# One layer pair on one core: gated one-hots on GpSimd, the sparse token tile chosen second, 111 row operations in the u loop, and an address strip in the expert stage

## The reference

```python
# experts: rows sorted by expert and padded to blocks of 128
def expert_block(args):
    xe, e = args
    gu = xe @ w_gate_up[e] + b_gate_up[e]
    g = jnp.minimum(gu[:, :D_FF], SWIGLU_LIMIT)
    u = jnp.clip(gu[:, D_FF:], -SWIGLU_LIMIT, SWIGLU_LIMIT)
    act = (u + 1.0) * (g * jax.nn.sigmoid(SWIGLU_ALPHA * g))
    return act @ w_down[e] + b_down[e]

# PEER: 8 heads choose 16 of 128 x 128 = 16384 experts per token
best_s, pos = lax.top_k(cand_s, PEER_TOPK)
expert_idx = jnp.take_along_axis(cand_i, pos, axis=-1)
gates = jax.nn.softmax(best_s, axis=-1)
u_sel = u_tab[i_blk]
act = jax.nn.gelu(jnp.einsum('td,thkd->thk', h_blk, u_sel).astype(jnp.float32))
w = (g_blk * act).astype(h.dtype)
return jnp.einsum('thk,thkd->td', w, v_tab[i_blk])
```

## Time and profile before

| | us |
|---|---|
| median of three runs | 3818.42 (3814.71 to 3826.18) |
| the profiled execution | 3818.46 |
| its span | 3816.6 |
| PE busy | 3387.5 (89%) |
| DVE busy | 2730.8 (72%) |
| ACT busy | 1932.5 (51%) |
| POOL busy | 607.7 (16%) |
| expert stage | from about 588 to 1815 |
| u loop | from about 2540 to 3222 |
| v loop | from about 3232 to 3802 |

### The profile page before, as it was taken

How to read it: one execution, slowest core, us unless ns; L and a number is a source line. 1 busy time by engine, 2 the same in 40 slices (tenths; PEclk the granted TensorE clock), 3 DMA queues, 4 the chain that set the end, 5 groups by cost and what they waited for, 6 DMA issues and landing times. The chain is left out here.

```text
span 3816.6 us, 46791 instructions
## 1 busy us (share of the span) xinstructions
PE 3387.5 (89%) x16253; PEld 2821.9 (74%) x16253; DVE 2730.8 (72%) x3557; ACT 1932.5 (51%) x2328; POOL 607.7 (16%) x428
## 2 busy tenths in 40 slices
PE   7697745999999999999299977799999987999998
PEld 3485544777777777777188856589999987777776
DVE  8316536999999999999544226337888766788887
ACT  1225414777777777777124334225878874332332
POOL 0000011001011011010200000000000254555652
PEclk9898867999999999999589978899999998999999
DMA  7520107999999999999633301134545689999997
GB/s 296 176 67 2 46 30 260 375 379 374 378 375 374 378 375 373 379 374 363 239 97 92 98 22 45 63 139 160 183 177 216 258 331 363 358 371 379 385 381 274
DMA packets 217467, 954.88 MB, mean 250 GB/s; under 512 B 23344, under 2 KB 85040, under 8 KB 142448
## 3 DMA queue, kind: packets, MB, share of 16 engines
q1 hardware_dynamic: 161872, 734.91, 52.0%
q0 software_dynamic: 46816, 167.80, 11.7%
q10 hardware_dynamic: 8640, 50.34, 3.2%
HBM read 864.92 MB, written 88.05 MB: 250 GB/s over the span
## 5 line engine op out<-in xcount | busy, mean ns | idle before, releaser
L1394 DVE TENSOR_TENSOR w_low<-w_raw,w_high 128x2048 fp32r<-128x2048 f32 x399 | 908.6, 2288 | 91.3 <-ACT w_high L1323 86.4
L1323 ACT ACTIVATE w_high<-w_raw 128x2048 fp32r<-128x2048 f32 x399 | 765.0, 1917 | 329.9 <-PE ps L125 182.3
L123 PE MATMUL ps<-w_high,xT_high 128*128 128x512 f32 x1056 | 433.6, 411 | 21.8 <-issue 21.8
L2462 DVE TENSOR_TENSOR uv_lo<-uv_raw,uv_hi 128x2048 fp32r<-128x2048 f32 x128 | 293.3, 2292 | 198.8 <-ACT uv_hi L2267 198.0
L124 PE MATMUL ps<-w_low,xT_high 128*128 128x512 f32 x1056 | 418.4, 396 | 0.0
L125 PE MATMUL ps<-w_high,xT_low 128*128 128x512 f32 x1056 | 418.1, 396 | 0.0
L123 PE MATMUL ps<-h4T_high,uv_hi 128*128 128x384 f32 x1024 | 355.9, 348 | 18.5 <-ACT a_out L2304 14.9
L123 PE MATMUL ps<-uv_hi,w_hi 128*128 128x512 f32 x768 | 306.3, 399 | 45.7 <-DVE w_lo L2477 34.8
L124 PE MATMUL ps<-h4T_low,uv_hi 128*128 128x384 f32 x1024 | 346.5, 338 | 0.0
L125 PE MATMUL ps<-h4T_high,uv_lo 128*128 128x384 f32 x1024 | 346.4, 338 | 0.0
L2267 ACT ACTIVATE uv_hi<-uv_raw 128x2048 fp32r<-128x2048 f32 x128 | 244.7, 1912 | 149.0 <-PE ps L125 119.2
(11 more groups left out here) (515 smaller groups left out, 6991.0 us busy)
## 6 DMA issues: line engine op xcount, KB each, us to landing
w_raw<-in_w_gate_up SPq DMA_DIRECT2D x267, 1024.0 KB, 6.9
w_raw<-in_w_down SPq DMA_DIRECT2D x132, 1024.0 KB, 6.9
uv_raw<-in_peer_u SPq DMA_DIRECT2D x64, 1024.0 KB, 5.3
uv_raw<-in_peer_v SPq DMA_DIRECT2D x64, 1024.0 KB, 9.3
wbuf_ada<-in_w_ada SPq DMA_DIRECT2D x12, 2048.0 KB, 8.8
a_rows<-a_out SPq DMA_DIRECT2D x128, 192.0 KB, 2.0
g_rows<-spread ACTq DMA_DIRECT2D x12, 2048.0 KB, 8.4
qT<-g_rows SPq DMA_DIRECT2D x16, 1536.0 KB, 15.1
```

The lines of the kernel that those rows point to most:

```text
L123: pe.matmul(out, l_hi, r_hi, start=first, stop=False)
L1323: act.activation(w_hi[:, n % SPLIT, :], w_raw[:, n % RAW, :], ACT.Copy).then_inc(s_wh, 1)
L1394: dve.tensor_tensor(w_lo[:, n % SPLIT, :], w_raw[:, n % RAW, :], w_hi[:, n % SPLIT, :].bitcast(F32), ALU.subtract).then_inc(s_wl, 1)
L2462: dve.tensor_tensor(uv_lo[:, n % 2, :], uv_raw[:, n % 2, :], uv_hi[:, n % 2, :].bitcast(F32), ALU.subtract).then_inc(s_lo, 1)
```

## The change

1. The four `first_hot` of a round are made by POOL, each in one operation (compare with the chosen key, times the gate). The operations of ScalarE (`gated_hots`) and of VectorE go, and `selT` keeps three planes for five, so that all tiles behind it in the peer stage lie 2048 bytes lower.
2. The sparse tile is selected second (`ORDER`, `SPARSE`), in steps 12 to 22. Its rows can be gathered from step 23 on. 111 row operations lie in the u loop: one a step in steps 24 to 45 (four in step 34), five a step from 46 to 59, four from 60 to 63. The v loop has 145 in place of 182. The rounds lie thinner in steps 12 to 33 and denser from 34 on (62 by step 45 in both), and the last ones come in step 59 for 58.
3. POOL follows the table: in step n the one-hots of its rounds, then the gathers whose buffers are worked off in step n (`gathers_at`). The buffers in `keysT` and `work` come in from gather 30 on (for 8), the one in `rows_c` from 112 (for 84).
4. In the expert stage an unused tile of 1728 bytes, `room_xT`, lies ahead of `xT_high`.

```diff
     xe = sb(stage, "xe", [P, D])
+    sb(stage, "room_xT", [P, 432])
     xT_hi, xT_lo = (sb(stage, f"xT_{x}", [P, 2, 4 * P], F32R) for x in ("high", "low"))
...
-    ORDER, SPARSE = (1, 2, 0, 3), 2
+    ORDER, SPARSE = (1, 0, 2, 3), 1
...
-    selT = sb(peer, "selT", [P, 2, 5, P])
+    selT = sb(peer, "selT", [P, 2, 3, P])
...
-    MIDDLE_AT, LATE_AT = 8, 84
+    MIDDLE_AT, LATE_AT = 30, 112
...
-    turns_at = {x: [at + k for k in range(11)] for x, at in enumerate((0, 12, 24, 35))}
-    hots_in = [[1] + [2] * 15 + [1], [2, 2, 2, 1] * 4 + [2, 2], [2, 3] * 6 + [2]]
-    hots_from = (11, 28, 46)
-    rows_in = {45: 2, 46: 4} | {n: 4 for n in range(47, NG)} | {NG + k: 3 if k % 9 else 2 for k in range(NG - 1)}
+    turns_at = {x: [at + k for k in range(11)] for x, at in enumerate((0, 12, 23, 35))}
+    hots_in = [[1, 1, 2] * 4 + [1, 1, 1, 2] * 2 + [2, 2, 2], [2, 3] * 6 + [2], [2, 3] * 6 + [2]]
+    hots_from = (11, 34, 47)
+    rows_in = {n: 1 for n in range(24, 47)} | {n: 5 for n in range(47, 60)} | {n: 4 for n in range(60, NG)}
+    rows_in |= {34: 4, 46: 5}
+    rows_in |= {NG + k: 3 if k % 3 == 0 else 2 for k in range(NG - 1)}
...
+    work_step = [n for n in range(2 * NG) for kind, x, c in plan[n] if kind == "S" for _ in range(c)]
+    first_step = max(turns_at[SPARSE]) + 1
+    gather_step = [work_step[before_of[g]] if before_of[g] >= 0 else first_step for g in range(2 * SEL)]
+    for g in range(2 * SEL):
+        if g >= MIDDLE_AT:
+            gather_step[g] = max(gather_step[g], max(turns_at[TT - 1]) + 1)
+        gather_step[g] = max(gather_step[g], gather_step[g - 1] if g else 0)
...
+            def hots(r):
+                s, tile = r % HOTS, 4 * r // P
+                if r * 4 % P == 0:
+                    pool.wait_ge(s_selh, tile + 1)
+                if r >= HOTS:
+                    pool.wait_ge(s_gb, r - HOTS + 1)
+                at = 4 * r % P
+                for q in range(4):
+                    pool.tensor_scalar(first_hot[:, s, q, :], iota_row[:, :], selT[:, tile % 2, 0, at + q:at + q + 1],
+                                       selT[:, tile % 2, 2, at + q:at + q + 1], ALU.is_equal, ALU.mult).then_inc(s_hotp, 1)
...
+            for n in range(2 * NG):
+                for kind, x, c in plan[n]:
+                    if kind == "H":
+                        for k in range(c):
+                            hots(x + k)
+                for g in gathers_at[n]:
+                    gather(g)
...
             def gate_products(r):
                 s = r % HOTS
-                pe.wait_ge(s_hot, 2 * (r + 1))
-                pe.wait_ge(s_hota, 3 * (r + 1))
+                pe.wait_ge(s_hot, r + 1)
+                pe.wait_ge(s_hotp, 4 * (r + 1))
...
-            def gated_hots(r):
...
-                for q in range(3):
-                    token = (4 * r + q) % P
-                    act.activation(first_hot[:, s, q, :], iota_row[:, :], ACT.Abs,
-                                   bias=selT[:, tile % 2, 3, token:token + 1]).then_inc(s_dist, 1)
...
-                dve.tensor_scalar(first_hot[:, s, 3, :], iota_row[:, :], selT[:, tile % 2, 0, at + 3:at + 4],
-                                  selT[:, tile % 2, 2, at + 3:at + 4], ALU.is_equal, ALU.mult).then_inc(s_hot, 1)
```

More of the change, by code:

```diff
@@ L2058, in emit @@
         sem(f"peer_{x}") for x in ("scores", "scores_read", "shifted", "exp", "selected", "sel_turned", "sel_here"))
-    s_hi, s_lo, s_used, s_pa, s_gelu, s_hot, s_dist, s_hota, s_gb, s_gt2, s_gst = (
-        sem(f"peer_{x}") for x in ("high", "low", "split_used", "dots", "gelu", "one_hots", "distances", "gated_hots", "gate_products",
+    s_hi, s_lo, s_used, s_pa, s_gelu, s_hot, s_hotp, s_gb, s_gt2, s_gst = (
+        sem(f"peer_{x}") for x in ("high", "low", "split_used", "dots", "gelu", "second_hots", "gated_hots", "gate_products",
                                    "gates_spread", "gates_stored"))
@@ L2104, in emit @@
     assert left == 0
+    work_step = [n for n in range(2 * NG) for kind, x, c in plan[n] if kind == "S" for _ in range(c)]
[5 more added lines that the diff above has]
+        gather_step[g] = max(gather_step[g], gather_step[g - 1] if g else 0)
+        assert gather_step[g] <= work_step[g]
     exp_at, sel_at, scores_at, count = {}, {}, {}, [0] * TT
@@ L2118, in emit @@
     places = [((), (3,), (2, 6), (1, 4, 7))[len(rounds)] for rounds in rounds_in]
+    gathers_at = [[g for g in range(2 * SEL) if gather_step[g] == n] for n in range(2 * NG)]
     turned_before = [sum(y != SPARSE for y in range(x)) for x in range(TT + 1)]
@@ L2126, in _, with gather @@
         def _(pool):
[L2127 to L2131, removed]
+            def hots(r):
[8 more added lines that the diff above has]
+                                       selT[:, tile % 2, 2, at + q:at + q + 1], ALU.is_equal, ALU.mult).then_inc(s_hotp, 1)
+            def gather(g):
+                if g == 0:
+                    pool.wait_ge(s_xr, 16)
+                    pool.wait_ge(s_sel, SPARSE + 1)
                 if g == MIDDLE_AT:
@@ L2141, in _ @@
                                         bass.IndirectOffsetOnAxis(ap=row_id[:, k:k + 1], axis=0)).then_inc(s_row[home_of[g]], 16)
+            u_table = t["peer_u_rows"]
+            v_table = t["peer_v_2"].rearrange("k n (j d) -> (k n j) d", d=D)
+            for n in range(2 * NG):
[5 more added lines that the diff above has]
+                    gather(g)
         @block.sync
@@ L2308, in take_selected @@
                 if tile >= 2:
-                    act.wait_ge(s_hot, 2 * (tile - 1) * P // 4)
+                    act.wait_ge(s_hotp, 4 * (tile - 1) * P // 4)
+                    act.wait_ge(s_hot, (tile - 1) * P // 4)
                 src = ps[:, 2, 0:3 * P].rearrange("p (c n) -> p c n", c=3)
-                act.activation(selT[:, tile % 2, 0:3, :], src, ACT.Copy)
-                act.activation(selT[:, tile % 2, 3:5, :], src[:, 0:3:2, :], ACT.Copy, scale=-1.0).then_inc(s_selh, 1)
+                act.activation(selT[:, tile % 2, :, :], src, ACT.Copy).then_inc(s_selh, 1)
             high(0)
@@ L2319, in _ @@
                     rounds, early = rounds_in[n], sum(at < 4 for at in places[n])
-                    coming = list(rounds_in[n + 1]) if n + 1 < NG else []
-                    if coming and n not in sel_at:
-                        gated_hots(coming.pop(0))
                     for r in rounds[0:early]:
@@ L2327, in _ @@
                         take_selected(turned_before[sel_at[n]])
-                    for r in coming:
-                        gated_hots(r)
                     for r in rounds[early:]:
@@ L2494, in _ @@
                     weights(n + 1 - NG)
-                    row_work(rows.pop(0))
+                    for g in rows[:1]:
+                        row_work(g)
                     weights_low(n + 1 - NG)
-                for g in rows:
+                for g in rows[1 if n >= NG else 0:]:
                     row_work(g)
```

## The result

| | before | after |
|---|---|---|
| median, us | 3816.57 of 4 runs (3814.23 to 3826.18) | 3902.27 of 4 runs (3901.16 to 3904.09) |
| ratio | | 1.022, 95% interval 1.0202 to 1.0239: slower |
| span of the profiled execution | 3816.6 | 3902.3 |

The ratios of the experiments further down are against the kernel before, run again beside each group of them (medians of 3817.5 to 3826.6 us), so a difference of a few us to the 3816.6 here says little.

The account below looks back on a forecast made before the run. TensorE was taken to bound the expert stage and u loop, with added DMA waits in the u and v loops. Strip -32, v loop -32 and u loop +14 gave -50, from 3818 to 3768 us, range 3740 to 3801.

Parts of the forecast that it names:

- Strip, -32: Expert stage: the strip brings matmuls from 233 to 226.5 ns apart, -32 us, ends 0 and -38.
- v loop, -32: v loop: some 40 fewer gathers relieve DMA, two thirds of 48 us regained, -32 us, ends -15 and -48.
- my two thirds: v loop: the share taken of 48 us lost to DMA, since g_rows bursts will still make someone late.
- u loop, +14: Late u loop: GpSimd needs 208 us for a stretch of 187, less some 8 us: +14, ends 0 and +89.
- The lower bound, the affine select at 0.29: Late u loop: least price of a GpSimd one-hot, 0.29 us, 37 us for 128, never binding.
- the upper, the copy at 1.13: Late u loop: highest price of a GpSimd one-hot, 1.13 us from a one-column copy beside busy VectorE, 145 us for 128.
- TensorE's lead: Late u loop: four buffers of one-hots and most of a step ahead save TensorE some 8 us once.
- Rounds before step 46: Early u loop: rounds are spread more evenly, and their 0.9 us each are the same wherever they lie.
- The rival "Slower": u loop steps 47 to 59: GpSimd becomes the bound as one-hots wait out VectorE, +89 us, whole 3843; chance 0.05.
- The chances: Whole kernel: forecast 0.60, strip without effect 0.14, v-loop gain given back 0.15, slower 0.05, better 0.06.

Follow-up runs that it names:

- e2: The changed kernel with the gated one-hots back on ScalarE (3 of 4) and VectorE (1 of 4): 3767.9 us, ratio 0.9867.
- e1: The kernel before with only the 1728-byte address strip added ahead of xT_high: 3786.2 us, ratio 0.9912.
- e10: e2 with the gates stored in 24 pieces of 16 tokens from two buffers of 8 KB: 3747.3 us, ratio 0.98.

## Why the prediction was wrong

- **Strip, -32.** Right: -29, alone and in company, with 227 ns where I expected 226.5. The cause that I gave, the distance's remainder, fits six more layouts, with 256 in place of 512.
- **v loop, -32.** Right in sign and mechanism: -40 (-37.5 in e2 against e1), which is five sixths of the 48 us for my two thirds. `a_rows` made VectorE wait 8.9 us for 52.4, so hardly anyone came late.
- **u loop, +14: the step that failed.** It was "I take a surplus of 0.3 and 0.6 us each: 77 us". A one-hot measured 1.37 us in the late u loop, of which 0.78 are its own and 0.59 waits, and the stretch that GpSimd set was 17 steps with 148 of them, not 15 with 128. At 0.6 us 148 are 89 us; they took 202, and these 113 us more are about what steps 46 to 63 lost (114). Both parts of my price were too low. The lower bound, the affine select at 0.29, was far from this operation; the upper, the copy at 1.13, was no upper bound at all, since a single one-hot takes up to 4.6 us in this window and 5.6 us elsewhere. I had the row that told of the waits, 0.94 against 1.68 us for a gather, and carried over its mean surplus of 0.53 us, then cut it to 0.3 because VectorE is idle a third of the time. The cut had no ground: measured, 0.59.
- **TensorE's lead, "some 8 us once".** The form was right: a lead is used up once. But beside what GpSimd took longer, 100 us in a window of 310 where e2 takes 210, it counts for little: TensorE stopped for 108 us.
- **Rounds before step 46, "the same wherever they lie".** Wrong for this kernel: without GpSimd's one-hots they cost 12 us (469.3 in e2 for 456.9 in e1), packed at 2.5 a step from step 34. But e10, which has e2's table, takes 456.9 us again, with 57 rounds of TensorE in these steps for e1's 60. So most of the 12 us is the wait for the stores of `g_rows`, which rounds this dense no longer hide, and not the rounds as such. GpSimd's one-hots add 22 (491.6). I had looked for GpSimd's bound only behind step 47; its queue had no gap over 0.7 us left from 2801 us on, just ahead of step 32. (The count of "62 by step 45 in both" was off, too: by `hots_in` 64 rounds are made by then before, and 62 after, so two more fall into the late stretch.)
- **The rival "Slower"** was what happened, one-hots that wait out VectorE's instructions and TensorE waiting at its rounds. I gave it +89, where +155 was measured, and a chance of 0.05. What I held against it, "VectorE would idle while it waits for POOL, and POOL would then be fast", was half true: VectorE was busy 151 of 310 us, and three one-hots in four took 0.78 to 1 us. The other quarter was enough.
- **The chances** leaned on one guess in the middle of an interval of four to one (0.29 to 1.13), whose upper part decided the sign: by my own sum it turned at 1.0 us. Even one-hots free of waits would have filled GpSimd for an estimated 226 us where e2 takes 210: there was no gain to be had in this stretch.

The Trainium skill ("SBUF — State Buffer", Who interferes with whom) has the rule that decides the case: a VectorE instruction with two SBUF inputs contends with a GpSimd instruction that reads SBUF, and one with a single input does not. The trace agrees with both halves: of the 151 one-hots that met a two-input instruction 94 took over 1 us, and the 93 that met only other VectorE instructions, most of them the selection's search through one tile, took 0.79 on average. I cited this rule and gave it 0.3 us.

## What to carry to other kernels

Before work goes to GpSimd, take its price with nothing beside it and add what VectorE's two-input instructions make it wait, chain by chain: a one-hot that begins inside one waits for the next one too, if that follows at once. Then sum the queue by step, gathers included, over the whole loop, and compare it with the time of a step; an engine at nine tenths of its time with others waiting is the bound, whatever lead its buffers give. Where two edits load one engine, run each alone: here the table gained 18 us and the one-hots cost 87, and both together cost 116. And where a matmul's pace differs between stages of one shape, look at the distance in SBUF between the tile it holds and the one it streams: here a multiple of 256 bytes gave 227 ns for 233.5.

## What the hardware did that I had not expected

- **Who began first decides, but a waiting one-hot is passed over.** The Trainium skill (same page, Summary: rules for kernel authors) says of such a pair that the second to issue blocks until the first is done. The trace agrees in part. 98 one-hots began inside a two-input instruction and took 2.53 us on average. 47 began at least 0.1 us ahead of one and kept their 0.79 us on average, 0.90 at most, and then VectorE paid: 13 of its instructions of 128x512 and more began 0.10 to 0.37 us into a one-hot and took 0.08 to 0.31 us longer than undisturbed (a subtraction 2.60 for 2.29). But the 32 that began later in it, with up to 0.3 us of it still to run, took 0.01 us longer on average. And where the next two-input instruction followed at once, the waiting one-hot was passed over in all 62 cases and outlasted that one too; in 29 of them it was done before the end of a later one in the same chain. That is how 0.78 us become 4.6.
- **A matmul's pace hangs on where tiles lie to each other**, by 6 ns in 233 in a stage of 1160 us. The Trainium skill ("SBUF — State Buffer", Who interferes with whom) says that TensorE never waits on anyone; this case's seven layouts differ all the same, and what in the hardware does it, no run here shows.
- **A stop costs more than its length.** After 8 us without work TensorE ran at half its pace from 3071.7 to about 3075.7 us, 0.32 us a matmul for 0.17, which is an estimated 2 us more for this stop; so late one-hots also slowed the work behind them.
